# Dense operands on 256-byte starts, and the scan's dt and gates projected feature-major

## The reference, cut to what matters

```
hn = _rmsnorm(h, norm1_g) * (1.0 + scale1) + shift1
w_z, w_xbc, w_dt, w_q, w_kc, w_vc, w_ks, w_vs, w_kw, w_vw, w_gn, w_gs, w_ga = jnp.split(w_in, offsets, axis=1)
# in the mixer: h_xbc = hn @ w_xbc, h_dt = hn @ w_dt (32 heads); hn @ w_gn (48 gates), hn @ w_vs, hn @ w_vw
dt = softplus(h_dt + dt_bias);  a = -exp(a_log)
# the scan, in 4 chunks of 128 tokens
acum = cumsum(dtc * a, axis=1)
decay = exp(where(tril, acum[:, :, None] - acum[:, None, :], -inf))
w_end = exp(acum[:, -1:] - acum) * dtc
new_state = state * exp(acum[:, -1]) + einsum(bc, w_end, xc)
```

## Time and profile before

| | before |
|---|---|
| runs, median (lowest to highest) | 2779.8 us (2777.95 to 2786.99) |
| profiled execution, its own time | 2776.12 us |
| its span, mean granted TensorE clock | 2774.0 us, 0.963 |
| PE busy | 2599.5 us (94%), 13,933 matmuls |
| VectorE, ScalarE, GpSimd busy | 55%, 35%, 12% |
| VectorE's evictions in the MLP's up tiles (L1220) | 32, mean 1223 ns |
| DMA | 347.56 MB, mean 125 GB/s |

### The profile page before, as it was taken

How to read it: one execution, slowest core, us unless ns; L and a number is a source line. 1 busy time by engine, 2 the same in 40 slices (tenths; PEclk the granted TensorE clock), 3 DMA queues, 4 the chain that set the end, 5 groups by cost and what they waited for, 6 DMA issues and landing times. The chain is left out here.

```text
span 2774.0 us, 34212 instructions
## 1 busy us (share of the span) xinstructions
PE 2599.5 (94%) x13933; PEld 2042.5 (74%) x13933; DVE 1513.6 (55%) x2159; ACT 972.9 (35%) x1349; POOL 334.6 (12%) x193
## 2 busy tenths in 40 slices
PE   8999999999999999999998998999999798989984
PEld 6777788888777777888886887887777565865542
DVE  4564555554636545645655654665765787355313
ACT  3346532222323464322222332333532487320001
POOL 0000004542200000313440000000000000011110
PEclk9999999999999999999999999999999898979997
DMA  4221143444222212443441322233343001258996
GB/s 140 86 62 61 61 134 107 140 138 137 84 79 74 72 46 76 137 137 106 137 137 61 107 81 80 92 92 103 122 148 118 16 2 77 94 225 358 419 419 248
DMA packets 256229, 347.56 MB, mean 125 GB/s; under 512 B 30532, under 2 KB 233540, under 8 KB 243396
## 3 DMA queue, kind: packets, MB, share of 16 engines
q1 hardware_dynamic: 247652, 324.83, 34.4%
q0 software_dynamic: 8320, 20.46, 2.0%
q10 hardware_dynamic: 96, 0.02, 0.0%
HBM read 328.99 MB, written 24.12 MB: 127 GB/s over the span
## 5 line engine op out<-in xcount | busy, mean ns | idle before, releaser
L199 PE MATMUL ps<-h_hi,w_hi 128*128 128x512 f32 x1728 | 695.0, 402 | 25.6 <-DVE h_lo L319 7.5
L201 PE MATMUL ps<-h_hi,w_lo 128*128 128x512 f32 x1728 | 678.9, 393 | 0.0
L200 PE MATMUL ps<-h_lo,w_hi 128*128 128x512 f32 x1728 | 678.7, 393 | 0.0
L176 ACT ACTIVATE w_hi<-w_raw 128x2048 fp32r<-128x2048 f32 (+1 forms) x168 | 316.8, 1886 | 784.4 <-PE ps L201 764.1
L181 DVE TENSOR_TENSOR w_lo<-w_raw,w_hi 128x2048 fp32r<-128x2048 f32 (+1 forms) x168 | 431.9, 2571 | 201.1 <-ACT w_hi L176 201.1
L199 PEld LDWEIGHTS ps<-h_hi,w_hi 128*128 128x128 f32 x1728 | 328.6, 190 | 106.7 <-issue 40.1
L200 PEld LDWEIGHTS ps<-h_lo,w_hi 128*128 128x128 f32 x1728 | 328.7, 190 | 69.4 <-issue 4.1
L201 PEld LDWEIGHTS ps<-h_hi,w_lo 128*128 128x128 f32 x1728 | 327.5, 190 | 70.1
L201 PE MATMUL ps<-merged_hi,w_lo 128*128 128x512 f32 x640 | 252.8, 395 | 0.0
L199 PE MATMUL ps<-merged_hi,w_hi 128*128 128x512 f32 x640 | 252.8, 395 | 0.0
L200 PE MATMUL ps<-merged_lo,w_hi 128*128 128x512 f32 x640 | 252.8, 395 | 0.0
(11 more groups left out here) (485 smaller groups left out, 3708.9 us busy)
## 6 DMA issues: line engine op xcount, KB each, us to landing
w_raw<-in_w_in SPq DMA_DIRECT2D x268, 256.0 KB, 3.6
w_raw<-in_w_up SPq DMA_DIRECT2D x128, 256.0 KB, 3.4
w_raw<-in_w_down SPq DMA_DIRECT2D x128, 256.0 KB, 3.6
room<-in_w_ada SPq DMA_DIRECT2D x96, 256.0 KB, 6.0
expert_over_h<-in_w_exp_down SPq DMA_DIRECT2D x10, 1024.0 KB, 26.1
w_raw<-in_w_out SPq DMA_DIRECT2D x32, 256.0 KB, 3.4
w_raw<-in_w_ssm_out SPq DMA_DIRECT2D x32, 256.0 KB, 3.6
expert_over_w<-in_w_exp_gate SPq DMA_DIRECT2D x8, 1024.0 KB, 19.0
```

The costliest lines, as they stand in the source:

```text
L176: act.activation(self.hi[:, q, :, 0:cols], raw[:, q, :, 0:cols], ACT.Copy).then_inc(self.hi_ready, 1)
L199: pe.matmul(out, w[0], x[0], start=start, stop=False)
L200: pe.matmul(out, w[0], x[1], start=False, stop=False)
L201: return pe.matmul(out, w[1], x[0], start=False, stop=stop)
```

## The change

**Part 1, starts.** Unused tensors (`gap`) are put in front: 224 bytes at the right end; 1184 and 1696 bytes ahead of merged_0 and merged_1; 672 ahead of yn; 1792 ahead of merged_two on the right; none ahead of h and of expert_over_h (`H_GAP` is 0). `vector_rows` (1024 bytes), used in the first block only, moves to the right side.

**Part 2, the small tile.** dt and the gates are projected with the weights stationary (80 columns) and h moving (512 columns), 24 matmuls, into features by tokens. ScalarE copies the result to `small_features`, PE transposes it in four pieces after the first token block of the value tile, and ScalarE copies those to dt_gates. dt's chain runs on VectorE and ScalarE beside the value tile; the two sums stand on PE after its third block, the decays after them. The values are copied to v_tokens in two halves. VectorE's two splits of z tiles at the end become one; the other, its ScalarE split and SP's last load go to the beginning of `ssd`. dt, dt_a, acum, decay_end and decay_all become tensors that live through both stages. In `ssd` dt's chain, the sums, the decays and the waits for them are gone.

```diff
+RIGHT_EDGE = 224
+H_GAP, MERGED_GAP, YN_GAP, TWO_GAP = 0, (1184, 1696), 672, 1792
...
+
+    if size:
+        ctx.enter_context(nc.sbuf_tensor(f"gap_{name}", [P, size // 4], F32, side=side))
+
+
...
+        gap(nc, ctx, "right_edge", RIGHT_EDGE, "right")
+        gap(nc, self.until_experts, "before_h", H_GAP, "right")
...
+            gap(self.nc, until_next, f"merged_{l}", MERGED_GAP[l])
...
+            small_turned, small_taken, values_half, ac_ready = (sem(x) for x in ("small_turned", "small_taken", "values_half", "ac_ready"))
+            prep, prep_a, dt_ready, acs_done, dl_ready = (sem(x) for x in ("prep", "prep_a", "dt_ready", "acs_done", "dl_ready"))
...
+            SMALL = SSM_HEADS + 3 * NH
+            small_t, v, ea = sb("small_features", [P, S]), sb("dt_v", [P, TB, SSM_HEADS]), sb("exp_a", [P, SSM_HEADS])
+            dt, dta, acs, dl, el = self.dt, self.dta, self.acs, self.dl, self.el
+            small_ps, turned_ps = self.pst[0:SMALL, 0, 0], self.pst[:, 0, 1, 0:TB * SMALL].rearrange("p (b n) -> p b n", b=TB)
+            values_ps = self.flat(4, TB * 2 * NKV).rearrange("p (b n) -> p b n", b=TB)
+            sums_ps = self.ps[:, 7, 0:2 * TB * SSM_HEADS].rearrange("p (a b h) -> p a b h", a=2, b=TB)
...
-                self.issue2(sp, P_XBC, P_Z)
+                self.issue2(sp, P_XBC, P_Z - 1)
+                W.issue(sp, B2 + P_Z + 1, 0, self.tile2(P_Z + 1, 0))
...
-                tile_tokens(pe, W, B2 + P_SMALL, 0, self.pst, self.h, SSM_HEADS + 3 * NH)
-                tile_tokens(pe, W, B2 + P_SMALL, 1, self.pst, self.h, 2 * NKV)
+                W.ready(pe, B2 + P_SMALL, 0)
+                for k in range(KC):
+                    mm = products(pe, small_ps, (W.hi[:, 0, k, 0:SMALL], W.lo[:, 0, k, 0:SMALL]), (self.h[0][:, k, :], self.h[1][:, k, :]), k == 0, k == KC - 1)
+                mm.then_inc(W.tile_done, 1)
+                W.ready(pe, B2 + P_SMALL, 1)
+                for b in range(TB):
+                    for k in range(KC):
+                        mm = products(pe, values_ps[:, b], (self.h[0][:, k, b * P:(b + 1) * P], self.h[1][:, k, b * P:(b + 1) * P]),
+                                      (W.hi[:, 1, k, :], W.lo[:, 1, k, :]), k == 0, k == KC - 1)
+                    if b == 0:
+                        pe.wait_ge(W.evicted[0], B2 + P_SMALL + 1)
+                        for a in range(TB):
+                            e = pe.transpose(turned_ps[:, a], small_t[0:SMALL, a * P:(a + 1) * P], self.c("ident")[0:SMALL, 0:SMALL])
+                        e.then_inc(small_turned, 1)
+                    if b == 1:
+                        mm.then_inc(values_half, 1)
+                    if b == 2:
+                        pe.wait_ge(dt_ready, 1)
+                        pe.matmul(sums_ps[:, 0], self.c("prefix"), dta[:], start=True, stop=True)
+                        pe.matmul(sums_ps[:, 1], self.c("ones"), dta[:], start=True, stop=True).then_inc(ac_ready, 1)
+                mm.then_inc(W.tile_done, 1)
...
-                for q, (to, w) in enumerate(((self.dtgn, SSM_HEADS + 3 * NH), (self.vsvw, 2 * NKV))):
-                    W.done(act, B2 + P_SMALL, q)
-                    tok = self.pst[:, q].rearrange("p a b -> p (a b)")[:, 0:TB * COL].rearrange("p (b n) -> p b n", b=TB)
-                    act.activation(to[:], tok[:, :, 0:w], ACT.Copy).then_inc(W.evicted[q], 1)
-                    W.split_hi(act, B2 + P_SMALL + 1, q)
+                act.preload_act_table_set(EXP_LN)
+                act.activation(ea[:], self.p2("alog"), ACT.Exp).then_inc(prep_a, 1)
+                W.done(act, B2 + P_SMALL, 0)
+                act.activation(small_t[0:SMALL, :], small_ps, ACT.Copy).then_inc(W.evicted[0], 1)
+                W.split_hi(act, B2 + P_SMALL + 1, 0)
+                act.wait_ge(small_turned, 1)
+                act.activation(self.dtgn[:], turned_ps, ACT.Copy).then_inc(small_taken, 1)
+                act.wait_ge(prep, 2)
+                act.activation(dt[:], dt[:], ACT.Exp).then_inc(prep_a, 1)
+                act.wait_ge(prep_a, 2)
+                act.activation(dt[:], dt[:], ACT.Ln, bias=1.0).then_inc(prep_a, 1)
+                act.wait_ge(values_half, 1)
+                act.activation(self.vsvw[:, 0:2], values_ps[:, 0:2], ACT.Copy)
+                act.wait_ge(dl_ready, 1)
+                act.activation(el[:], sums_ps[:, 1], ACT.Exp)
+                act.activation(dl[:], dl[:], ACT.Exp)
+                W.done(act, B2 + P_SMALL, 1)
+                act.activation(self.vsvw[:, 2:4], values_ps[:, 2:4], ACT.Copy).then_inc(W.evicted[1], 1)
...
-                for q in range(2):
-                    W.split_lo(dve, B2 + P_SMALL + 1, q)
+                bias = self.p2("dtb").unsqueeze(1).to_broadcast([P, TB, SSM_HEADS])
+                dve.wait_ge(small_taken, 1)
+                dve.tensor_tensor(v[:], self.dtgn[:, :, 0:SSM_HEADS], bias, ALU.add).then_inc(prep, 1)
+                dve.wait_ge(prep, 1)
+                dve.scalar_tensor_tensor(dt[:], v[:], -1.0, v[:], ALU.mult, ALU.min).then_inc(prep, 1)
+                dve.wait_ge(prep_a, 3)
+                dve.scalar_tensor_tensor(dt[:], v[:], 0.0, dt[:], ALU.max, ALU.add).then_inc(prep, 1)
+                dve.wait_ge(prep, 3)
+                dve.scalar_tensor_tensor(dta[:], dt[:], -1.0, ea[:].unsqueeze(1).to_broadcast([P, TB, SSM_HEADS]), ALU.mult, ALU.mult).then_inc(dt_ready, 1)
+                W.split_lo(dve, B2 + P_SMALL + 1, 0)
+                dve.wait_ge(ac_ready, 1)
+                dve.tensor_copy(acs[:], sums_ps[:, 0]).then_inc(acs_done, 1)
+                dve.wait_ge(acs_done, 1)
+                dve.tensor_tensor(dl[:], sums_ps[:, 1], acs[:], ALU.subtract).then_inc(dl_ready, 1)
...
-            (prep, prep_a, dt_ready, acs_done, dl_ready, we_ready, ac_ready, half, taken0) = (sem(x) for x in (
-                "prep", "prep_a", "dt_ready", "acs_done", "dl_ready", "we_ready", "ac_ready", "half_done", "half_taken"))
+            half, taken0 = sem("half_done"), sem("half_taken")
...
-            dt, dta, v, ea = sb("dt", [P, TB, SSM_HEADS]), sb("dt_a", [P, TB, SSM_HEADS]), sb("dt_v", [P, TB, SSM_HEADS]), sb("exp_a", [P, SSM_HEADS])
-            acs, dl, el = (sb(x, [P, TB, SSM_HEADS]) for x in ("acum", "decay_end", "decay_all"))
+            dt, dta, acs, dl, el = self.dt, self.dta, self.acs, self.dl, self.el
...
-            small = self.ps[:, 7, 0:2 * TB * SSM_HEADS].rearrange("p (a b h) -> p a b h", a=2, b=TB)
...
+                W.issue(sp, B2 + P_Z + 1, 1, self.tile2(P_Z + 1, 1))
...
-                    if n == 1:
-                        pe.wait_ge(dl_ready, 1)
-                        pe.wait_ge(we_ready, 1)
...
-                pe.wait_ge(dt_ready, 1)
-                pe.matmul(small[:, 0], self.c("prefix"), dta[:], start=True, stop=True)
-                pe.matmul(small[:, 1], self.c("ones"), dta[:], start=True, stop=True).then_inc(ac_ready, 1)
...
-                act.preload_act_table_set(EXP_LN)
-                act.activation(ea[:], self.p2("alog"), ACT.Exp).then_inc(prep_a, 1)
-                act.wait_ge(prep, 2)
-                act.activation(dt[:], dt[:], ACT.Exp).then_inc(prep_a, 1)
-                act.wait_ge(prep_a, 2)
-                act.activation(dt[:], dt[:], ACT.Ln, bias=1.0).then_inc(prep_a, 1)
...
+                W.split_hi(act, B2 + P_Z, 1)
...
-                act.wait_ge(ac_ready, 1)
-                act.wait_ge(acs_done, 1)
-                act.activation(el[:], small[:, 1], ACT.Exp).then_inc(we_ready, 1)
-                act.wait_ge(dl_ready, 1)
-                act.activation(dl[:], dl[:], ACT.Exp).then_inc(we_ready, 1)
...
-                        if G == 0:
-                            dve.wait_ge(we_ready, 2)
...
-                bias = self.p2("dtb").unsqueeze(1).to_broadcast([P, TB, SSM_HEADS])
-                dve.tensor_tensor(v[:], self.dtgn[:, :, 0:SSM_HEADS], bias, ALU.add).then_inc(prep, 1)
-                dve.wait_ge(prep, 1)
-                dve.scalar_tensor_tensor(dt[:], v[:], -1.0, v[:], ALU.mult, ALU.min).then_inc(prep, 1)
-                dve.wait_ge(prep_a, 3)
-                dve.scalar_tensor_tensor(dt[:], v[:], 0.0, dt[:], ALU.max, ALU.add).then_inc(prep, 1)
-                dve.wait_ge(prep, 3)
-                dve.scalar_tensor_tensor(dta[:], dt[:], -1.0, ea[:].unsqueeze(1).to_broadcast([P, TB, SSM_HEADS]), ALU.mult, ALU.mult).then_inc(dt_ready, 1)
-                dve.wait_ge(ac_ready, 1)
-                dve.tensor_copy(acs[:], small[:, 0]).then_inc(acs_done, 1)
-                dve.wait_ge(acs_done, 1)
-                dve.wait_ge(we_ready, 1)
-                dve.tensor_tensor(dl[:], small[:, 1], acs[:], ALU.subtract).then_inc(dl_ready, 1)
...
+                W.split_lo(dve, B2 + P_Z, 1)
...
+            gap(nc, st, "yn", YN_GAP)
...
-        self.vector_rows = self.sb("vector_rows", [P, 2, P])
+        self.vector_rows = self.until_first.enter_context(self.nc.sbuf_tensor("vector_rows", [P, 2, P], F32, side="right"))
...
```

(10 more changed lines are left out.)

## The result

| | before | after |
|---|---|---|
| median of the runs (lowest to highest) | 2779.0 us (2777.95 to 2786.99), 4 runs | 2735.91 us (2733.67 to 2740.01), 4 runs |
| ratio of the two, 95% interval | | 0.984 (0.9818 to 0.9863) |
| span of the profiled execution, granted clock | 2774.0 us, 0.963 | 2735.0 us, 0.967 |
| PE busy | 2599.5 us | 2570.6 us (94%) |

What follows compares the result with a forecast made beforehand. TensorE's stream of matmuls was taken to bound the kernel. Starts 99 us less 5 of waits, 94, plus 15 for the small tile made 109 us: 2776.1 to 2667, stated as 2669, range 2646 to 2724.

Steps and rivals of the forecast that it cites:

- rival E: Dense products: moving and stationary operands both at 0 conflict, h pays 6.5 ns more, 2797 us; chance 0.05.
- its term of 54 us: Products with h moving: 5,184 less some 75, each 10.6 ns faster from a start at 0, 54.2 us saved.
- The value of 216 ns: Pace taken for an aligned 512-column product: 213.3 ns plus the 3 ns of the fp32 rows.
- Rival B: Dense products: a start at 0 is no better than 224; merged and yn gain 15 us, h nothing; 2749 us; chance 0.08.
- the 39.4 forecast: Products with merged and yn moving: 2,304, each 17.1 ns faster from a start at 0, 39.4 us saved.
- the 5.1 us forecast: Savings from new starts: merged_two's products 2.0 us, the 256-column products 3.1 us.
- A: Dense products: a start at 0 removes half the loss, h to 221 and merged to 225 ns; 2716 us; chance 0.17.
- C: MLP and attention stages: pace falls as forecast but PE then waits, 40% of part 1 lost; 2706 us; chance 0.08.
- D: Dense products: the new starts do nothing, the unit that counts being 32 bytes or less, or tensors land elsewhere; 2763 us; chance 0.06.
- Forecast 15 us: Small tile to the scan: dt and gates feature-major, dt's chain out of the scan; 15 us saved, between 10 and 19.
- gap at the scan: PE's idle time before the scan: from 7.6 us to 3.3 us, as 0.3 + 0.6 + 2.4.
- clock: Behind two new 3.3 us gaps, stretches at 1.2 GHz costing between nothing and 3 us each; 3.4 us for both.

Runs made afterwards that it cites:

- w128_h0: The changed kernel with w alone at 128 bytes past a multiple of 256, h and the other moving operands at 0; 2779.0 us.
- all128: The changed kernel with every dense operand (w, h, merged, yn, merged_two) at 128 bytes past a multiple of 256; 2739.3 us.
- bench_b: The changed kernel with bursts of 24 matmuls added at the projection stage's start, varying operand starts, load widths, banks and bf16; fp32r 226.7 ns at best, bf16 215.8.
- p1_only: The kernel before the change with the new starts alone; 2758.7 us against 2776.5 on the same chip, ratio 0.9939.
- after_again: The changed kernel run once more, unaltered, for comparison on one chip with a reordered version; 2735.5 us.
- bench_a: The changed kernel with bursts of 24 fp32r matmuls added at the projection stage's start, varying the moving operand's start and both widths; 226.7 ns at distance 0.
- p2_only: The changed kernel with all gaps 0, so the small-tile part alone with the old starts; 2758.0 us against 2776.5, ratio 0.9938.
- map_a: The changed kernel, w and h at 0, with merged_0 at 32, merged_1 at 64, yn at 96 and merged_two at 128 bytes; 2751.4 us.
- map_b: The changed kernel, w and h at 0, with merged at 160 and 192, yn at 128 and merged_two at 224 bytes; 2749.7 us.
- reorder: The changed kernel with the value tile's w_hi and w_lo and the features' copy put ahead at the projection stage's end; 2734.7 us, repeated 2737.1 beside 2735.5 unaltered.

## Why the prediction was wrong

**The step that failed.** "So the pace depends on where the moving operand starts." The three rows bear this out only as long as one looks at the moving operand: h and merged_two at 224, merged at 96. But w lay at 224 too, and the same rows say as well that equal starts are fast and unequal ones slow. I wrote that equality down, as an argument against rival E, and did not draw its consequence: if the distance counts, h has nothing to gain from a new start, since w moves with it. w128_h0 and all128 show the distance to be what counts; h stayed at 226.7 and its term of 54 us was 0. The 256-column products had stood at distance 0 as well, and w128_h0 shows that they don't mind it anyway.

**The value of 216 ns.** It came from the lower clock and from the fp32 rows, which lose next to nothing, and led to the belief that 13.3 ns at 2.4 GHz were a fault of the starts. They aren't: 226.7 ns is what an fp32r product with its own 128-column load takes at the best start found. Neither row was of that kind. One was at 1.2 GHz; in the other each of the two passes takes 428 ns at 2.4 GHz, so there too a column enters at half the rate of an fp32r product. That the cost is absent at half the rate said nothing of what a start can save at the full one. (The printed rows give 428 and 430 ns by the recorded working, where the trace's finer times are 426.7 and 428.6; nothing hangs on it.) The page "TensorE: Matmul & The Clock Gate", Wait — 56ns, not 53.3ns?, of the Trainium skill, whose 215.8 ns the prediction had put aside, is right for what it says: bench_b has 215.8 in bf16. It doesn't hold for fp32r, where this chip takes 226.7.

**Merged and yn.** Rival B, with a chance of 0.08, had the mechanism: 2,304 products x 6.6 ns = 15.2 us for the 39.4 forecast, and h nothing; the two merged stages alone show 12.7 us of it, and p1_only's median 17.8. Its time of 2749 is still 13 us above the measured 2736. Of these, the traces place 4.6 in part 2 and 2.1 behind the scan's end; the rest is spread over medians and stretches too uncertain to place. merged_two and the 256-column products gained nothing, for the 5.1 us forecast.

**Rivals A, C, D, E.** A has the wrong shape: h did not move, and merged is now level with it. C never came to the test. At 226.7 ns the MLP tile keeps its 10.9 us, and VectorE fits as before, with 4.96 us for w_lo and 3.42 for merged_lo where the earlier trace rows have 5.24 and 3.41. PE's waits for `room` in the attention stages went from 5.4 us to 6.3, which is no change: other traces of kernels with after's paces have 5.4 (all128) to 7.1 (after_again). D is wrong in size, since the first part is worth 15 to 18 us. The page "SBUF — State Buffer", Specifications (TRN2), of the Trainium skill, on which it drew, gives 16-byte cachelines; bench_a has 226.7 at 0 and 229.8 to 234.0 at 32 and more bytes, all of them whole lines, so that rule is not what counts here. E's mechanism is the reverse of the truth: both at the same place is the best case, not a conflict.

**Part 2.** Forecast 15 us; 19.6 between the small tile's first product and the scan's second step, and 18.5 by p2_only's median. Term by term, after against forecast: small tile 5.6 us for 5.2 (233.5 ns, not 216); wait for w_lo 2.9 for 3.3; value tile with transposes and sums 12.3 for 11.7 (120 ns, not 112); gap at the scan 1.1 for 3.3; the scan's first step 5.6 for 5.3; clock 0 for 3.4. Their sum is 27.5 for 32.2. Two terms were mis-sized. The gap: I carried the 2.4 us between the last w_lo and the scan over from before as a fixed cost. By the times of its queue it was SP that ended last, not VectorE. The timeline of SP's queue before, and after:

```profile
1653.25 27.45 SPq L169 DMA_DIRECT2D w_raw<-in_w_in  x12
```

```profile
1625.33 22.37 SPq L179 DMA_DIRECT2D w_raw<-in_w_in  x12
```

Before, SP's last issue waited for a w_lo and ended at 1680.70, 0.4 us ahead of the scan's start at 1681.14. After, the issue that the change moves into the scan is no longer there, and SP's last one ends at 1647.7, ahead of PE. The last to end is ScalarE's copy of half the values, as forecast (timeline of ScalarE in after):

```profile
1650.26 0.60 ACT L1620 ACTIVATE v_tokens<-ps 128x512 f32<-128x512 f32 x1 [1.75 <-PE ps L211]
```

It ends at 1650.86, and the scan starts 0.3 us later, not 2.4. The prediction named the moved issue and saw no one waiting for it. The clock: I had charged 3.4 us for the two gaps without a row that prices one; neither trace of after has a drop there, and p2_only, w128_h0, all128, map_a and map_b lose 1.4 or 1.5 us behind the wait for w_lo, in the same order of work. That after loses nothing is luck. That the drops of before are gone counts in the small tile and in the scan's first step, 10.8 us before and 5.6 now.

## What to carry to other kernels

With fp32r operands look at the distance between the starts of the moving and the stationary operand, not at the address of either: with 512 moving columns 0 modulo 256 bytes gave 226.7 ns, nearly every other distance 229 to 234, and a start 4 bytes past was the worst. With 256 moving columns a distance of 128 cost nothing. One gap in the wrong place (w alone by 128 bytes) cost 43 us of 2736. Before costing a pace at less than any row shows, ask whether the rows that reach the ideal are of the same kind of operand, clock and passes; a burst of 24 products in the kernel's own trace settles it.

And at the end of a stage follow every engine's last instruction, the DMA issuer's among them: what is last there is what the next stage waits for.

## What was not expected of the hardware

- fp32r, 128 stationary and 512 moving columns: 226.7 ns at best, 13.4 over one column per cycle at 2.4 GHz, 13.3 at 384 and 256 columns, nothing at 1.2 GHz (426.7); bf16 215.8 at the four distances tried.
- The distance between the operands' starts costs fp32r products of 512 moving columns 2 to 11 ns, and those of 256 nothing (distances 0 and 128).
- Narrower stationary operands are slower, not faster: 229.0 to 233.2 ns for 112 to 32 columns at distance 0.
- 192 and 128 moving columns both step by 110 ns.
- After a change of distance a stream takes up to ten products to settle at 226.7 ns.
- Behind one and the same 5.0 us wait, before has nine of the next stage's products at 1.2 GHz and reorder eight; after, whose work lies 3 us later than reorder's, has none. That is worth 2.1 and 1.7 us.
